# Second mixer's pairs: outputs summed with channels in partitions, and the small inverse as a product of crossed powers

## The chip, the cores and the metric

One core of one Trainium2 chip. The metric is the device time of one execution of the whole program, in microseconds (us). Between kernels the medians of repeated executions are compared.

## The reference, cut to what matters

The program is two blocks. The change lies in the second block's first mixer, a recurrence over 512 tokens in 16 heads of 64 channels, with one 64x64 state for each head:

```python
def rwkv7_time_mix(xn, mu, w_in, w0, w1, w2, a0, a1, a2, k_k, k_a, r_k, lnx_g, lnx_b, w_out):
    ...
    def step(state, inp):
        r_t, w_t, k_t, v_t, kk_t, a_t = inp
        s_kk = jnp.einsum('bhij,bhj->bhi', state, kk_t)
        state = (state * w_t[:, :, None, :]
                 - s_kk[..., None] * (kk_t * a_t)[:, :, None, :]
                 + v_t[..., None] * k_t[:, :, None, :])
        return state, jnp.einsum('bhij,bhj->bhi', state, r_t)
    ...
    mean = jnp.mean(y, axis=-1, keepdims=True)
    var = jnp.mean(jnp.square(y - mean), axis=-1, keepdims=True)
    y = ((y - mean) * lax.rsqrt(var + GN_EPS) * lnx_g.astype(f32).reshape(H, N)
         + lnx_b.astype(f32).reshape(H, N))
    y = y + jnp.sum(r * k * r_k.astype(f32), axis=-1, keepdims=True) * v
    y = y.reshape(B, S, D).astype(xn.dtype) * jax.nn.silu(g)
    return y @ w_out
```

## The kernel before, in words

The kernel takes the heads two at a time: eight **pairs** `p` of 128 channels. Within a pair the tokens are cut into eight **chunks** of 64. Inside a chunk the recurrence is turned into matrix products, which needs the inverse of a 64x64 triangular matrix for each chunk and head, 16 to a pair. The state passes from chunk to chunk.

A tile of 16 such 64x64 matrices has 128 partitions and eight blocks of 64 columns. The upper and the lower 64 partitions are the even and the odd chunk of two, and a block is one head of such a two. All products of such tiles are float32, 64 rows deep and 64 columns wide, so that one takes a quarter of the array of TensorE. There are two kinds:

- `blocks_pe` (line 2758): 16 products, each from upper half to upper half or from lower to lower. They land in one PSUM bank. Only two of the four quarters of the array are used.
- the crossed kinds, `to_heads_pe` (2776), `from_heads_pe` (2788), `TaT_pe` (2999) and `channels_pe` (2800): 16 products that go from chunk halves to head halves or back, by turns in all four quarters. They land in two banks.

For each pair the steps are, by their names in the code:

1. `C1`, `C2`, `MT` (line 2800) and VectorE's masks (`mask_dve`, 3478) that take them to `M`, `qb`, `qk`, `ak`, `MT`, `O16` and `O32`.
2. The inverse of the 16x16 diagonal blocks by squaring: `N` and `NT` (second powers), `MT2` and `M2` (fourth), `NT3` (eighth), each a `blocks_pe` that ScalarE copies to SBUF (3166). Each power is multiplied onto the running `X` by `X0`, `X1`, `X2`, also `blocks_pe`, and added to `X` by VectorE (`add_X_dve`, 3562). Then `T16`, `G16`, `A16` and `T32`, `G32`, `A32` widen the inverse to 32 and to 64.
3. `WX`, `Wv`, `TaT`: what the state is multiplied with.
4. The recurrence, for each chunk `c`: `from_state_pe` (3015, 3017) reads the state `St`; VectorE makes `nU` (3584) and copies the part of the output that comes from the state into `yt` (3595); `to_state_pe` (3032, 3034) makes the update; VectorE scales the old state (`SP`, 3605) and forms the new one (`S`, 3615).
5. `inside_pe` (3050, 3053): the rest of the output of all eight chunks, 32 small products in a row into bank 7, with tokens in partitions. `inside_dve` (3754) adds it to `yt`, `turn_y_pe` transposes the sum (4 transposes, 288), and `yf_act` (3398) copies it.
6. `mean` (3072), `dv` (3764), `y2` (3406), `var` (3080), then `sd`, `normed` (3773), `gain` (3432), `add_bonus` (3782), `out` (3791).

The order of the work is written out by hand, one list for each engine: `pair_pe`, `pair_act` and `pair_dve`, called for `s` from 0 to 10. They interleave the pairs. Between `TaT` of one pair and `TaT` of the next, TensorE carries the eight chunks of pair `s - 1`, and between its two halves of every chunk one step of item 1 or 2 for pair `s`; then it goes on to `inside`, `T16`, and so on. A **from `TaT` to `TaT`** stretch is called an interval here; there are seven. Before the first one only pair 0's matrices are made. After the last one `EarlyOut` fills the gaps of pair 7's chunks with matmuls of the output projection (3921), and what is left of them follows.

Each engine runs its list in order. A wait (`wait_ge`) holds all that stands behind it on that engine. `K.bank(b, ...)` lets TensorE wait until the last reader of a PSUM bank is done. For instance `N` waits for `O32`, the last reader of `MT` in banks 0 and 1, and `tal` and `tka` wait for whoever reads their bank before.

Of the kernel before, what the change touches and what calls it, by code (L numbers as in the profile page):

```python
# [2685 lines left out]
class Pairs:  # L2686
    def __init__(self, K):
        blocks = lambda: K.carve(8, HEAD)
        two = lambda: [blocks() for _ in range(2)]
        self.nU, self.yt = two(), two()  # L2690
# [179 lines left out]
def NT_pe(K, X, q, p):  # L2870
# [4 lines left out]
    blocks_pe(K, q, p, "NT", X.M, X.MT, q.act)  # L2875


def X0_pe(K, X, q, p):
    if outside(p):
        return  # L2880
    K.nc.tensor.wait_ge(*q.act.at("NT read", p))
    K.nc.tensor.wait_ge(*q.dve.at("X start", p))
    blocks_pe(K, q, p, "X0", X.NT, X.X, q.dve)


def M2_pe(K, X, q, p):
# [4 lines left out]
    blocks_pe(K, q, p, "M2", X.NT, X.N, q.act)  # L2891


def MT2_pe(K, X, q, p):
# [4 lines left out]
    blocks_pe(K, q, p, "MT2", X.N, X.NT, q.act)  # L2899


def X1_pe(K, X, q, p):
    if outside(p):
        return
    K.nc.tensor.wait_ge(*q.act.at("MT2 read", p))
    K.nc.tensor.wait_ge(*q.dve.at("X0 read", p))
    blocks_pe(K, q, p, "X1", X.MT, X.X, q.dve)
# [1922 lines left out]
```

## Time and profile before

| | us |
|---|---|
| median of 3 executions | 2651.22 (2648.41 to 2654.54) |
| profiled execution, its own time | 2643.84 |
| its span | 2642.2 |
| TensorE (PE) busy in the span | 2504.9 (95%) |
| first `C2` of pair 0 to `TaT` of pair 0 | 1832.30 to 1855.02 |
| the seven intervals | 1855.02 to 2081.45 |
| from there to the end of the early output matmuls | 2081.45 to 2126.5 |

The stretch that the change touches is thus some 295 us of 2642. In the rows PE is TensorE's matmuls, DVE is VectorE, ACT is ScalarE. A float32 matmul is recorded as two, so that a product of 16 shows as x32.

### The profile page before, as it was taken

How to read it: one execution, taken by the hardware profiler on the slowest of the kernel's cores; microseconds unless marked ns; L12 is line 12 of the kernel's file. 1: busy time of each engine (PE TensorE's matmuls, PEld its weight loads, DVE VectorE, ACT ScalarE, POOL GpSimd, SP SyncE). 2: the span in 40 equal slices, each digit the busy share in tenths (PEclk: the TensorE clock that was granted, in tenths of full speed). 3: DMA queues.
4: the chain of work that ended last, by engine and by line, in shares of the span. 5: the costliest groups of instructions: out<-in, count | busy, mean ns of one | idle time of the engine just before them, and what ended most of it. 6: DMA issues, size and time to landing. Idle time of an engine off the chain costs nothing. (4 is left out here: it accounts for less than half of the span.)

```text
span 2642.2 us, 43397 instructions
## 1 busy us (share of the span) xinstructions
PE 2504.9 (95%) x17508; PEld 1694.5 (64%) x17508; DVE 1295.2 (49%) x2714; ACT 678.5 (26%) x1184; POOL 166.2 (6%) x128
## 2 busy tenths in 40 slices
PE   8999999999999899899998989999999899999997
PEld 3666676488874667666665644865777645677644
DVE  4656656567653222122121127622787535666625
ACT  2333233101112111111111111023455323333422
POOL 0000000000000012222222210000000000000000
PEclk9999999999999899999999999999999999999999
DMA  6222112244342598999999882342111142111120
GB/s 276 113 80 96 64 48 76 92 167 182 121 158 80 233 370 320 387 335 395 381 347 394 311 326 98 100 183 97 34 62 34 54 171 74 64 57 57 64 76 32
DMA packets 83733, 436.54 MB, mean 165 GB/s; under 512 B 16432, under 2 KB 16944, under 8 KB 39888
## 3 DMA queue, kind: packets, MB, share of 16 engines
q1 hardware_dynamic: 54592, 372.92, 35.8%
q0 software_dynamic: 18096, 37.80, 5.6%
q10 hardware_dynamic: 10848, 23.04, 2.4%
q8 instruction: 141, 2.31, 0.4%
q14 instruction: 56, 0.46, 0.0%
HBM read 400.59 MB, written 61.41 MB: 175 GB/s over the span
## 5 line engine op out<-in xcount | busy, mean ns | idle before, releaser
L278 PE MATMUL psum_all<-u,weights 128*128 128x512 f32 x704 | 306.9, 593 | 0.0
L278 PEld LDWEIGHTS psum_all<-u,weights 128*128 128x128 f32 x704 | 132.4, 190 | 157.7 <-issue 157.3
L958 PE MATMUL psum_all<-big,weights 128*128 128x256 f32 x928 | 214.7, 381 | 2.1 <-ACT sq L1015 1.3
L1892 PE MATMUL psum_all<-big 128*32 128x256 f32 (+2 forms) x1648 | 195.1, 382 | 6.0 <-DMA big<-t_experts 4.5
L958 PEld LDWEIGHTS psum_all<-big,weights 128*128 128x128 f32 x928 | 174.5, 190 | 34.2 <-issue 5.1
L1892 PE MATMUL psum_all<-weights,big 128*64 128x256 f32 (+2 forms) x1296 | 187.9, 388 | 8.4 <-DMA weights<-t_experts 8.4
L958 PE MATMUL psum_all<-big 128*128 128x256 f32 x784 | 179.0, 379 | 0.0
L1892 PEld LDWEIGHTS psum_all<-big 128*32 128x32 f32 (+2 forms) x1648 | 138.1, 132 | 39.0 <-issue 8.8
L958 PEld LDWEIGHTS psum_all<-big 128*128 128x128 f32 x784 | 148.7, 190 | 22.4 <-DVE big L946 0.8
L1892 PEld LDWEIGHTS psum_all<-weights,big 128*64 128x64 f32 (+2 forms) x1296 | 131.2, 145 | 48.8 <-issue 15.4
L1927 DVE COPY big<-psum_all 128x256 f32<-128x256 f32 x46 | 19.5, 424 | 279.1 <-PE psum_all L288 279.1
L278 PE MATMUL psum_all<-weights,u 128*128 128x256 f32 x640 | 139.6, 379 | 0.0
L278 PEld LDWEIGHTS psum_all<-weights,u 128*128 128x128 f32 x640 | 121.5, 190 | 19.9 <-issue 3.8
L1902 ACT ACTIVATE big<-psum_all 128x256 f32<-128x256 f32 x46 | 17.7, 385 | 442.2 <-PE psum_all L1892 421.1
L1939 PE MATMUL psum_all<-weights,big 128*32 128x512 f32 (+2 forms) x440 | 110.3, 633 | 12.7 <-DMA weights<-t_experts 7.5
L288 PE MATMUL psum_all<-const_cols,big 128*128 128x128 f32 (+2 forms) x748 | 108.2, 278 | 11.5 <-DMA big<-u_rows,rows 5.7
L278 PEld LDWEIGHTS psum_all<-big 128*128 128x128 f32 x568 | 78.8, 198 | 61.1 <-issue 50.3
L288 PEld LDWEIGHTS psum_all<-const_cols,big 128*128 128x128 f32 (+2 forms) x748 | 84.1, 141 | 46.4 <-issue 21.7
L278 PE MATMUL psum_all<-big 128*128 128x3 f32 (+4 forms) x568 | 92.0, 289 | 12.7 <-issue 5.6
L1939 PE MATMUL psum_all<-big 128*64 128x512 f32 (+2 forms) x296 | 95.8, 627 | 8.2 <-DMA big<-t_experts 6.8
L1961 DVE COPY big<-psum_all 128x512 f32<-128x512 f32 x35 | 24.2, 691 | 150.7 <-PE psum_all L1939 120.7
L2457 PE MATMUL psum_all<-big,weights 128*128 128x512 f32 x192 | 83.0, 592 | 3.6 <-DVE big L2611 3.6
(475 smaller groups left out, 4013.7 us busy)
## 6 DMA issues: line engine op xcount, KB each, us to landing
big<-t_experts SPq DMA_DIRECT2D x96, 1024.0 KB
weights<-t_experts SPq DMA_DIRECT2D x96, 1024.0 KB
weights<-t_ada SPq DMA_DIRECT2D x24, 1024.0 KB, 7.0
weights<-t_rkvg SPq DMA_DIRECT2D x16, 1024.0 KB, 8.6
rwkv_inputs<-big ACTq DMA_DIRECT2D x48, 256.0 KB, 2.3
big<-rwkv_inputs SPq DMA_DIRECT2D x8, 1280.0 KB, 6.8
weights<-t_x SPq DMA_DIRECT2D x8, 1024.0 KB, 4.9
weights<-t_BC SPq DMA_DIRECT2D x8, 1024.0 KB, 4.9
```

What stands on the lines that cost most here:

```text
L278: last = pe.matmul(out, lhsT, rhs, start=n == 0, stop=n == len(terms) - 1)
L288: last = K.nc.tensor.transpose(out, a, K.c("ident")[0:a.shape[0], 0:a.shape[0]])
L958: ins = pe.matmul(out, w[:, k, :], x[:, k, :], start=first and k == 0, stop=k == n - 1, skip_group_check=not first)
L1892: ins = pe.matmul(K.psum[rows, bank, n * F_E:(n + 1) * F_E], xT[:, k, rows], X.part(r, n, KD, F_E)[:, k, :], start=k == 0, stop=k == KD - 1)
L1902: act.activation(X.act[b % 2], K.psum[:, b % 2, 0:F_E], ACT.Silu).then_inc(*q.act.tick("gate", b))
L1927: dve.tensor_copy(X.hidT[b % 2].rearrange("p a b -> p (a b)"), K.psum[:, 4, 0:F_E]).then_inc(*q.dve.tick("hidT", b))
L1939: ins = pe.matmul(K.psum[rows, 2 + half, :], X.hidT[b % 2][:, j, rows], X.part(r, 2, 2, D)[:, j, half * 512:half * 512 + 512], start=j == ...
L1961: dve.tensor_copy(X.y[e % len(X.y)][:, 512:1024], K.psum[:, 3, :]).then_inc(*q.dve.tick("y", e))
L2457: ins = pe.matmul(K.psum[:, j % 4, :], K.W.tile(w, KD, 256)[:, k, j % 2 * P:(j % 2 + 1) * P], X.mix[c][:, k, :], start=k == 0, stop=k == K ...
```

## The change

Three things are changed.

**Outputs.** `yt`, its eight copies, `inside_dve` and `turn_y` go. `from_state_pe` makes the output's part with the operands swapped, so that channels are in partitions, straight into bank 6 (`Y_BANK`), and leaves the sum open. `inside_pe` now runs for each chunk, behind `to_state`, and adds its four products to it. Chunk 7's stands at the head of the next step. The update of the state moves from bank 6 to a part of bank 4. `from_state_pe` has two signals in place of one ("from S" after the first two products, "y from S" after the other two), and TensorE now also waits for two signals of its own: "y" of the chunk before and "y from S".

**Inverse.** In place of three additions of `power * X` it is a product: `P = (1 + M4)(1 + M)`, `Q = (1 + N) P`, `X = (1 + M8) Q`, where `A2`, `A4` and `A8` are the powers with the unit matrix added by VectorE. `N`, `NT`, `MT2`, `M2`, `NT3`, `P` and `X` are of the crossed kind, `Q` is `blocks_pe`.

**Order.** `WX` moves from chunk 2 to chunk 4, and its read behind `N`'s; `qb` moves behind `MT` on VectorE; on ScalarE `yf` and `gain` now stand behind `X`'s read and ahead of `T16`'s.

```diff
@@ class Pairs
-        self.nU, self.yt = two(), two()
+        self.nU = two()
@@
-        self.alt, self.Wv, self.WX = blocks(), blocks(), blocks()
+        self.alt, self.Wv, self.WX, self.A2, self.A4 = (blocks() for _ in range(5))
@@
-               "C2": 0, "C1": 2, "MT": 0, "WX": 2, "NT": 3, "N": 0, "X0": 1, "MT2": 2, "M2": 3,
-               "X1": 0, "NT3": 1, "tal": 2, "tka": 3, "X2": 0}
+               "C2": 0, "C1": 2, "MT": 0, "NT": 2, "N": 0, "WX": 2, "MT2": 0, "M2": 2,
+               "P": 0, "NT3": 2, "tal": 1, "Q": 0, "tka": 1, "X": 2}
@@ N_pe, NT_pe; M2_pe and MT2_pe likewise with from_heads_pe
-    blocks_pe(K, q, p, "N", X.MT, X.M, q.act)
+    to_heads_pe(K, q, p, "N", X.MT, X.M, q.act)
@@
+def P_pe(K, X, q, p):
...
+    for name in ("X start", "A4"):
+        K.nc.tensor.wait_ge(*q.dve.at(name, p))
+    to_heads_pe(K, q, p, "P", X.A4, X.X, q.act)
+def Q_pe(K, X, q, p):
...
+    K.nc.tensor.wait_ge(*q.act.at("P read", p))
+    K.nc.tensor.wait_ge(*q.dve.at("A2", p))
+    blocks_pe(K, q, p, "Q", X.A2, X.N, q.act)
+def X_pe(K, X, q, p):
...
+    K.nc.tensor.wait_ge(*q.act.at("Q read", p))
+    K.nc.tensor.wait_ge(*q.dve.at("NT3 read", p))
+    from_heads_pe(K, q, p, "X", X.M, X.NT, q.act)
@@ from_state_pe
+        K.bank(Y_BANK, q.act, "yf", p)
...
-        pe.matmul(K.psum[rows, 4 + h, 0:HEAD], chunk(X.TaT, c)[half(h), :], X.St[half(h), :], start=True, stop=True)
+        ins = pe.matmul(K.psum[rows, 4 + h, 0:HEAD], chunk(X.TaT, c)[half(h), :], X.St[half(h), :], start=True, stop=True)
+    ins.then_inc(*q.pe.tick("from S", p, c))
+    if c > 0:
+        pe.wait_ge(*q.pe.at("y", p, c - 1))
     for h in range(2):
-        ins = pe.matmul(K.psum[rows, 4 + h, HEAD:P], al_rh(X, p, c)[half(h), 1, :], X.St[half(h), :], start=True, stop=True)
-    ins.then_inc(*q.pe.tick("from S", p, c))
+        ins = pe.matmul(chunk(K.psum[half(h), Y_BANK, :], c), X.St[half(h), :], al_rh(X, p, c)[half(h), 1, :], start=True, stop=False)
+    ins.then_inc(*q.pe.tick("y from S", p, c))
@@
-def inside_pe(K, X, q, p):
+def inside_pe(K, X, q, p, c):
...
+    pe.wait_ge(*q.dve.at("nU", p, c))
+    pe.wait_ge(*q.pe.at("y from S", p, c))
+    for h in range(2):
+        pe.matmul(chunk(K.psum[half(h), Y_BANK, :], c), X.nU[n][rows, 2 * t + h, :], X.qb[n][rows, 2 * t + h, :],
+                  start=False, stop=False)
+    for h in range(2):
+        ins = pe.matmul(chunk(K.psum[half(h), Y_BANK, :], c), X.vt[n][rows, 2 * t + h, :], X.qk[n][rows, 2 * t + h, :],
+                        start=False, stop=True)
+    ins.then_inc(*q.pe.tick("y", p, c))
-def turn_y_pe(K, X, q, p):
...
@@ VectorE: A2_dve; A4_dve alike from X.MT; yt_dve and inside_dve are removed
+    dve.wait_ge(*q.act.at("NT read", p))
...
+    dve.tensor_tensor(X.A2, X.NT, K.c("eye64").unsqueeze(1).to_broadcast([P, 8, HEAD]), ALU.add).then_inc(*q.dve.tick("A2", p))
+def A8_dve(K, X, q, p):
...
+    dve.wait_ge(*q.pe.at("NT3", p))
+    dve.tensor_tensor(heads_first(X.M), crossed(K, "NT3"), K.c("eye64").unsqueeze(1).unsqueeze(1).to_broadcast([P, 2, NT, HEAD]),
+                      ALU.add).then_inc(*q.dve.tick("NT3 read", p))
@@ pair_act
-    NT3_act(K, X, q, s - 1)
-    expn_act(K, X, q, s)
+    P_act(K, X, q, s - 1)
     rate_act(K, X, q, s)
     tal_act(K, X, q, s - 1)
+    Q_act(K, X, q, s - 1)
+    expn_act(K, X, q, s)
+    tka_act(K, X, q, s - 1)
+    X_act(K, X, q, s - 1)
+    yf_act(K, X, q, s - 2)
     gain_act(K, X, q, s - 3)
-    tka_act(K, X, q, s - 1)
+    T16_act(K, X, q, s - 1)
+    G16_act(K, X, q, s - 1)
     expp_act(K, X, q, s)
-    T16_act(K, X, q, s - 1)
-    yf_act(K, X, q, s - 2)
-    G16_act(K, X, q, s - 1)
     y2_act(K, X, q, s - 2)
@@ pair_dve, the middle
-    add_X_dve(K, X, q, s - 1, "X0")
+    A2_dve(K, X, q, s - 1)
     S_dve(K, X, q, s - 2, 5)
-    scan_dve(K, X, q, s)
+    A4_dve(K, X, q, s - 1)
     nU_dve(K, X, q, s - 2, 5)
     SP_dve(K, X, q, s - 2, 5)
...
+    scan_dve(K, X, q, s)
+    S_dve(K, X, q, s - 2, 6)
+    SP_dve(K, X, q, s - 2, 6)
+    A8_dve(K, X, q, s - 1)
     ends_dve(K, X, q, s - 1)
```

The order on TensorE at chunks 6 and 7. Before (2758 is `NT3`, 3015 and 3017 `from_state`, 288 `tal` and `tka`, 3032 and 3034 `to_state`, 2758 again `X2`, and 3050 and 3053 the first of the eight like pairs of rows of `inside`):

```order
L2758 MATMUL psum_all<-weights 64x64 x16
L3015 MATMUL psum_all<-big 64x64 x2
L3017 MATMUL psum_all<-big 64x64 x2
L288 MATMUL psum_all<-const_cols,big 128x128 x4
L3032 MATMUL psum_all<-big 64x64 x2
L3034 MATMUL psum_all<-big 64x64 x2
L288 MATMUL psum_all<-const_cols,big 128x128 x4
L3015 MATMUL psum_all<-big 64x64 x2
L3017 MATMUL psum_all<-big 64x64 x2
L2758 MATMUL psum_all<-weights 64x64 x16
L3050 MATMUL psum_all<-big,weights 64x64 x2
L3053 MATMUL psum_all<-big,weights 64x64 x2
```

The same place after the change, from `tal` on (3019 and 3024 are `from_state`, 3039 and 3041 `to_state`, 3057 and 3060 `inside`, 288 `tal` and `tka`, 2758 `Q`, 2788 `X`):

```order
L288 MATMUL psum_all<-const_cols,big 128x128 x4
L3039 MATMUL psum_all<-big 64x64 x2
L3041 MATMUL psum_all<-big 64x64 x2
L3057 MATMUL psum_all<-weights,big 64x64 x2
L3060 MATMUL psum_all<-weights,big 64x64 x2
L2758 MATMUL psum_all<-weights,big 64x64 x16
L3019 MATMUL psum_all<-big 64x64 x2
L3024 MATMUL psum_all<-big 64x64 x2
L288 MATMUL psum_all<-const_cols,big 128x128 x4
L2788 MATMUL psum_all<-weights 64x64 x16
L3057 MATMUL psum_all<-weights,big 64x64 x2
L3060 MATMUL psum_all<-weights,big 64x64 x2
```

The last step of the small inverse is now a crossed product, and one chunk's `inside` stands in front of `T16` where all eight stood.

ScalarE at the same place, before (3166: read of `tal`; 3432 `gain`; 3166 read of `tka`; 3350 `expp`; 3166 read of `T16`; 3398 `yf`; 3173 read of `G16`; 3406 `y2`):

```order
L3166 ACTIVATE big<-psum_all 128x512
L3432 ACTIVATE big<-big,vector_cols 128x512
L3166 ACTIVATE big<-psum_all 128x512
L3350 ACTIVATE big<-big 128x512
L3166 ACTIVATE weights<-psum_all 128x512
L3398 ACTIVATE big<-psum_all 128x512
L3173 ACTIVATE weights<-psum_all 128x2x4x64
L3406 ACTIVATE big<-big 128x512
```

and after (reads of `tal` and `Q`, 3378 `expn`, reads of `tka` and `X`, 3415 `yf`, 3449 `gain`, reads of `T16` and `G16`, 3367 `expp`, 3423 `y2`):

```order
L3170 ACTIVATE big<-psum_all 128x512
L3170 ACTIVATE weights<-psum_all 128x512
L3378 ACTIVATE big<-big 128x512
L3170 ACTIVATE big<-psum_all 128x512
L3177 ACTIVATE weights<-psum_all 128x2x4x64
L3415 ACTIVATE big<-psum_all 128x512
L3449 ACTIVATE big<-big,vector_cols 128x512
L3170 ACTIVATE weights<-psum_all 128x512
L3177 ACTIVATE weights<-psum_all 128x2x4x64
L3367 ACTIVATE big<-big 128x512
L3423 ACTIVATE big<-big 128x512
```

`gain` moved from ahead of `tka`'s read to behind `X`'s read and `yf`, and three reads (`Q`, `tka`, `X`) with `expn` between stand ahead of it.

## Rows read from the trace of the kernel before

**Rows 1.** The page's first line.

```profile
span 2642.2 us, 43397 instructions
```

**Rows 2.** Busy time by stretch: four of the seven intervals; after the comma PE, PEld, DVE, ACT.

```profile
1855.02:1886.83 31.81, 29.60 (x796) 24.26 (x797) 24.25 (x59) 15.79 (x28) 0.00 (x0) 1.00 0.13 45
...
1918.98:1950.88 31.90, 29.78 (x797) 24.48 (x797) 26.23 (x62) 17.12 (x30) 0.00 (x0) 1.00 0.16 53
1950.88:1984.00 33.12, 29.91 (x796) 24.45 (x797) 26.46 (x62) 17.11 (x30) 0.00 (x0) 1.00 0.15 51
...
2049.27:2081.45 32.18, 28.39 (x790) 23.81 (x791) 22.58 (x56) 12.81 (x22) 0.00 (x0) 1.00 0.20 72
```

**Rows 3.** Timeline of TensorE, third interval: start, us, line, shapes, idle before.

```profile
1918.98 0.69 PE L2999 MATMUL psum_all<-weights,big 64*64 64x64 f32 x32 [0.32 <-ACT big L3388]
1919.47 1.13 PE L2758 MATMUL psum_all<-big,weights 64*64 64x64 f32 x32
1920.44 0.33 PE L3015 MATMUL psum_all<-big 64*64 64x64 f32 x4
...
1922.67 0.33 PE L3032 MATMUL psum_all<-big 64*64 64x64 f32 x4 [0.64 <-DVE big L3595]
...
1922.99 1.10 PE L2800 MATMUL psum_all<-big 64*64 64x128 f32 x32
1924.05 0.33 PE L3015 MATMUL psum_all<-big 64*64 64x64 f32 x4
...
1924.29 0.69 PE L2800 MATMUL psum_all<-big 64*64 64x64 f32 x32
1925.30 0.33 PE L3032 MATMUL psum_all<-big 64*64 64x64 f32 x4 [0.31 <-DVE big L3584]
...
1941.26 0.66 PE L288 MATMUL psum_all<-const_cols,weights 128*128 128x128 f32 x4
1942.20 0.63 PE L288 MATMUL psum_all<-const_cols,big 128*128 128x128 f32 x4 [0.28 <-DVE big L3754]
1942.76 0.69 PE L2776 MATMUL psum_all<-weights 64*64 64x64 f32 x32
...
1946.15 1.13 PE L3080 MATMUL psum_all<-big,const_cols 128*128 128x512 f32 x2 [0.38 <-ACT big L3406]
```

**Rows 4.** Groups of instructions by line and form, the pairs' stretch.

```profile
L3166 ACT ACTIVATE weights<-psum_all 128x512 f32<-128x512 f32 x56 | 33.5, 598 | 40.1 <-PE psum_all L2758 26.8 <-PE psum_all L3017 6.8 <-PE psum_all L288 6.2
...
L3595 DVE COPY big<-psum_all 64x128 f32<-64x128 f32 x64 | 18.1, 282 | 0.5
...
L3630 DVE TENSOR_TENSOR_SCAN big<-big 128x512 f32<-128x512 f32 x7 | 8.5, 1214 | 0.0
```

**Rows 5.** Timeline of ScalarE and of VectorE, third interval, the output's tail.

```profile
1939.84 0.82 ACT L3432 ACTIVATE big<-big,vector_cols 128x512 f32<-128x512 f32 x1 [0.99 <-DVE big L3773]
...
1941.97 0.68 DVE L3782 TENSOR_TENSOR big<-big 128x512 f32<-128x512 f32 x1
1942.76 0.69 DVE L3791 TENSOR_TENSOR u<-big 128x512 f32<-128x512 f32 x1
1943.37 0.69 DVE L3657 TENSOR_TENSOR big<-big 128x512 f32<-128x512 f32 x1
1944.75 0.69 DVE L3764 SCALAR_TENSOR_TENSOR big<-psum_all,big 128x512 f32<-128x512 f32 x1 [0.69 <-PE psum_all L3072]
```

**Rows 6.** Timeline of TensorE, the first pair before any recurrence.

```profile
1847.42 0.63 PE L288 MATMUL psum_all<-const_cols,weights 128*128 128x128 f32 x4 [0.88 <-DVE weights L3562]
```

**Rows 7.** Timeline of TensorE, pair 7's last chunk and what follows.

```profile
2099.40 0.33 PE L3015 MATMUL psum_all<-big 64*64 64x64 f32 x4
...
2100.48 0.33 PE L3050 MATMUL psum_all<-big,weights 64*64 64x64 f32 x4 [0.63 <-DVE big L3595]
...
2102.49 1.12 PE L3921 MATMUL psum_all<-u,weights 128*128 128x512 f32 x2
...
2108.35 18.19 PE L3921 MATMUL psum_all<-u,weights 128*128 128x512 f32 x42
```

More of the change, by code:

```diff
@@ L2874, in NT_pe @@
         K.nc.tensor.wait_ge(*q.dve.at(name, p))
[L2875 to L2883, printed above, removed]
+    to_heads_pe(K, q, p, "NT", X.M, X.MT, q.act)
 def M2_pe(K, X, q, p):
@@ L2898, in MT2_pe @@
         K.nc.tensor.wait_ge(*q.act.at(name, p))
[L2899 to L2907, printed above, removed]
+    from_heads_pe(K, q, p, "MT2", X.N, X.NT, q.act)
 def NT3_pe(K, X, q, p):
@@ L2935, in G16_pe @@
         return
-    for name in ("O16", "X2 read"):
-        K.nc.tensor.wait_ge(*q.dve.at(name, p))
-    to_heads_pe(K, q, p, "G16", X.O16, X.X)
+    K.nc.tensor.wait_ge(*q.dve.at("O16", p))
+    K.nc.tensor.wait_ge(*q.act.at("X read", p))
+    to_heads_pe(K, q, p, "G16", X.O16, X.X, q.act)
 def A16_pe(K, X, q, p):
@@ L3058, in turn_y_pe @@
-def turn_y_pe(K, X, q, p):
-    if outside(p):
-        return
-    K.nc.tensor.wait_ge(*q.dve.at("y", p))
-    K.bank(7, q.act, "yf", p)
-    transposes(K, [(tile(K.psum[:, 7, :], t), X.yt[p % 2].rearrange("p b n -> p (b n)")[:, t * P:(t + 1) * P]) for t in range(NT)]) \
-        .then_inc(*q.pe.tick("turn y", p))
+    pe, n, rows, t = K.nc.tensor, p % 2, half(c % 2), c // 2
+    if c == 0:
+        pe.wait_ge(*q.act.at("tv read", p))
+        for name in ("qb", "qk"):
+            pe.wait_ge(*q.dve.at(name, p))
@@ L3123, in pair_pe @@
     to_state_pe(K, X, q, s - 1, 0)
+    inside_pe(K, X, q, s - 1, 0)
     early.pe(s == KD, 1)
@@ L3238, in MT2_act, with P_act, Q_act, X_act @@
         K.nc.scalar.wait_ge(*q.pe.at(name, p))
-    take_act(K, q, p, "MT2", X.MT)
-def NT3_act(K, X, q, p):
+    take_crossed_act(K, q, p, "MT2", X.MT)
+def P_act(K, X, q, p):
     if outside(p):
         return
-    for name in ("X0", "MT2", "M2"):
+    for name in ("M2", "MT2"):
         K.nc.scalar.wait_ge(*q.pe.at(name, p))
-    take_act(K, q, p, "NT3", X.NT)
+    take_crossed_act(K, q, p, "P", X.N)
+def Q_act(K, X, q, p):
+    if outside(p):
+        return
+    K.nc.scalar.wait_ge(*q.dve.at("A2", p))
+    take_act(K, q, p, "Q", X.NT)
+def X_act(K, X, q, p):
+    if outside(p):
+        return
+    K.nc.scalar.wait_ge(*q.pe.at("P", p))
+    take_crossed_act(K, q, p, "X", X.X)
 def T16_act(K, X, q, p):
@@ L3252, in T16_act @@
         return
-    for name in ("X1", "NT3"):
-        K.nc.scalar.wait_ge(*q.pe.at(name, p))
+    K.nc.scalar.wait_ge(*q.pe.at("NT3", p))
+    K.nc.scalar.wait_ge(*q.dve.at("A4", p))
     take_act(K, q, p, "T16", X.MT)
@@ L3585, in nU_dve @@
                              X.Wv[rows, 2 * t:2 * t + 2, :], ALU.mult, ALU.subtract).then_inc(*q.dve.tick("nU", p, c))
-def yt_dve(K, X, q, p, c):
-    if outside(p):
-        return
-    dve, rows, t = K.nc.vector, half(c % 2), c // 2
-    if c == 0 and p >= 2:
-        dve.wait_ge(*q.pe.at("turn y", p - 2))
-    dve.wait_ge(*q.pe.at("from S", p, c))
-    dve.tensor_copy(X.yt[p % 2][rows, 2 * t:2 * t + 2, :], K.psum[rows, 4:6, HEAD:P]).then_inc(*q.dve.tick("from S read", p, c))
 def SP_dve(K, X, q, p, c):
@@ L3711, in rh_dve @@
     if p >= 2:
-        for key in (("C1", p - 2), ("C2", p - 2), ("from S", p - 2, 7)):
+        for key in (("C1", p - 2), ("C2", p - 2), ("y from S", p - 2, 7)):
             dve.wait_ge(*q.pe.at(*key))
```

150 lines of the change are left out of this document (68 added, 82 removed).

## The prediction

> **What bounds the kernel now.** I read the page first for the span [rows 1], then the busy time by stretch [rows 2], then the timelines of the three engines over one clean interval [rows 3, 5], and the groups of instructions [rows 4] for what one costs. The change touches only the pairs, so the question is what sets the length of an interval. In the third one, 31.90 us long, TensorE is busy 29.78, VectorE 26.23 and ScalarE 17.12 [rows 2]. The clock is granted in full (1.00). TensorE's idle time is a handful of short waits: 0.64 and 0.31 for VectorE in chunks 0 and 1, 0.28 for `inside_dve`, 0.38 for `y2`, 0.32 ahead of `TaT` [rows 3]. So TensorE's list is the bound, with VectorE 3.5 us behind it. The fourth interval is 1.2 us longer with the same busy time [rows 2]: gaps in issuing that wait for no engine. I leave those as they are. The profiled execution took 2643.84 us against a median of 2651.22; I work out a difference and take it off the median.
>
> **TensorE's sum.** Starts give the price of a product. `TaT`, crossed, lets the next start after 1919.47 - 1918.98 = 0.49; `Wv`, of the blocks kind, after 1920.44 - 1919.47 = 0.97 [rows 3]. Both hold the same 16 products. In an interval:
> - `X0`, `X1`, `X2` go: 3 x 0.97 = 2.91.
> - `N`, `NT`, `MT2`, `M2`, `NT3` become crossed: 5 x 0.48 = 2.40.
> - `P`, `X` (0.49 each) and `Q` (0.97) come: 1.95.
> - `turn_y` goes: 1942.76 - 1942.20 = 0.56 [rows 3].
> - `inside` took 2102.49 - 2100.48 = 2.01 in one run [rows 7]. As eight pieces, each costs what four small products cost in front of a like-shaped one, 1924.29 - 1924.05 = 0.24 [rows 3], so 1.9 to 2.1: nothing either way.
>
> Together -3.9 us. VectorE loses three additions, `inside_dve` and eight copies of 0.28 [rows 4], which stand 0.2 apart, and gains `A2`, `A4`, `A8`: about -2.3. ScalarE loses one read and gains three of 0.60 [rows 4], +1.2. If busy time decided, an interval would fall to 28 us.
>
> **Why it will not.** A crossed product takes 0.49, its read 0.60 on ScalarE [rows 3, 4]; until now a product of 0.97 covered it. The chain now also runs through more hands: `MT2` read, `A4`, `P`, its read, `Q`, its read, `X`, its read, `T16`. I walked the new lists through the third interval with the rows' durations: 0.61 from the start of one 512-wide VectorE operation to that of the next, 0.79 where it needs the result of the one before [rows 5], 0.5 between ScalarE's reads, and about 0.05 from an end to the start that waits. Times from `TaT`:
> - `to_state` 0 stays at 3.69; VectorE's list ahead of it is unchanged [rows 3].
> - `inside` 0 pushes `C1` from 4.01 to 4.21. `M` and `nU` 1 follow `C1`, so `to_state` 1 goes from 6.32 [rows 3] to 6.50: the first waits are not shortened.
> - `to_state` 2 at 8.95 waits for `nU`, behind `MT`'s and `qb`'s masks; `WX` no longer covers it.
> - `N` must wait for `O32` to leave banks 0 and 1: 10.40. `to_state` 4 comes at 13.1.
> - `P` waits for `A4`, behind `WX`'s, `kk2`'s and `MT2`'s reads on ScalarE: 15.1, after some 0.7 idle.
> - The scan (1.21 [rows 4]) and `A8` now stand ahead of `nU` 6: `to_state` 6 at 18.1.
> - `Q` 18.6, `from_state` 7 at 19.5, `tka` 19.8, `X` 20.45 (it waits for `Q`'s read). `X`'s read is behind `expn` and `tka`'s read: 21.3 to 21.9. `T16` starts at 21.95, before at 1941.26 - 1918.98 = 22.28.
>
> So of 3.9 us some 0.3 arrive at `T16`. Then the output's tail decides. After `X`'s read ScalarE does `yf` (0.5) and `gain` (0.82 [rows 5]), to 23.15. `add_bonus`, `out`, `k2`, `dv` follow on VectorE, whose starts lie 0.79, 0.61 and 0.61 apart [rows 5] (before, `dv` had to wait for `mean`; here `mean` is done first): `dv` ends at 25.9, `y2` at 26.55, and `var` starts at 26.62. Before, it started at 1946.15 - 1918.98 = 27.17 [rows 3]. From `var` to the next `TaT` the lists are as they were: 4.73, TensorE's own work. New interval: 31.35, **-0.55**.
>
> The other pieces. The first interval has no `gain`, `add_bonus` and `out`, so `dv` follows `mean` at once: -1.35. The last has no `k2`, and `gain` weighs as before: -1.15. Pair 0 before its `TaT` has no state work to cover anything, and is a chain of reads: by the same walk `T16` starts at 1847.9 instead of 1847.42 [rows 6], +0.5. At the end, pair 7's chunks grow by 0.1 each (`inside` stands on the way, `nU` may start 0.12 earlier), +0.7, and behind them 2.01 of `inside` become 0.3, `turn_y` goes, and the wait for `yt`'s copy shortens: the last run of output matmuls starts 1.65 earlier than 2108.35 [rows 7], and they are TensorE's own time.
>
> Sum: +0.5 - 1.35 - 5 x 0.55 - 1.15 - 1.65 = -6.4. From 2651.22: **2644.8 us**. Per interval the unknown is large beside its value: one operation more or less in the chain is 0.6. Ends: all of TensorE's 3.9 arrives, or `T16` comes 0.6 later and nothing does.
>
> A rule that speaks against the change: the Trainium skill, "TensorEngine Tiling (Array Packing)", section "PSUM Bottleneck", says that splitting the array speeds up TensorE but not the emptying of PSUM, which may then become the limit. By that rule the 3.9 us are not to be had, and the walk agrees; without it the intervals alone would give -27.
>
> **Rivals.**
> 1. *TensorE stays the bound.* The reads fit behind `inside`'s pieces after all. For it: VectorE has 2.3 us less to do, ScalarE is half idle [rows 2]. Against: the chain above, and that each engine takes its list in order. 7 x -3.9, and -1.65 at the end: about -29, 2622. Something halfway, -1.5 in each, gives 2638. Together 0.13.
> 2. *No change to measure.* The chain to `T16` is one operation (0.6) longer than I walk it, say because `A4` or `A8` slips behind the scan's turn. Then the intervals give nothing and only the ends help: -2 to -3, 2649. Chance 0.25.
> 3. *Slower: TensorE waits for itself.* Before, it never waited for its own signals here. Now each chunk has two, "y" of the chunk before and "y from S". The trace shows no such wait; a lower bound is nothing, since one product lies between the signal and the wait in nearly all cases; an upper one is what the last of a run of small products takes from its start to its end, 0.22 (the 0.69 of a set against its 0.49 spacing [rows 3]), and the signal's way of 0.05. 15 waits x 0.27 = 4 us in each pair, +26 in all with the gain taken off: 2677. At a third of it, 2655.5. It turns the sign from 0.05 us in a wait on (6.4 over 8 pairs and 15 waits). Chance 0.13, since the products that stand between last longer than 0.27.
> 4. *The crossed order does not run in four quarters for these tiles.* Then 7 products cost 0.48 more each and all waits behind them too; TensorE's sum is -0.6 and the sign turns. Against: `N` uses the very loop of `G16`. Chance 0.02.
>
> The Trainium skill, "TensorE: Matmul & The Clock Gate", section "The cost: per-tile semaphore tail", has increments serialize, some 26 ns for each. The change adds 14 signals to a pair. By that page alone this would be an estimate of +3 us in all and bring the sum to -3.4; the trace has no pair of places that differ in their signals alone, so the sum leaves it out. It would add to rival 3.
>
> **The numbers.** About 0.2% (5.3 us) is what a measurement of this kernel can tell from no change. My forecast is 2644.8 with a chance of 0.47, spread over -3 to -11: its middle is just beyond the bound, so some 0.41 of it and all of rival 1 are faster (0.54). The other 0.06, rival 2 and a quarter of rival 3 are within it (0.34), the rest of rival 3 and rival 4 slower (0.12). The range goes from halfway to rival 1's milder case and beyond to rival 3 at a third and the medians' own spread: 2631 to 2656.
>
> **What would show it.** Right: the intervals with about 31.3 us and TensorE busy some 26 in them; waits of TensorE for ScalarE's reads ahead of `P` and `T16`, for VectorE ahead of `N`; `dv` started by VectorE's own list and not by `mean`; `var` the only late step after it. `turn_y` gone and the run after `var` earlier by 1 to 2. Wrong in favour: intervals under 30. Wrong against: idle time of TensorE at lines 3024 and 3057 with no other engine named, or `inside`'s pieces over 0.3 each.

## The result: slower, 1.0067 times the kernel before, and the profile after

Measured together, 11 executions of each: **2673.59 us** (median, 2659.59 to 2679.14) against 2652.0 before. The ratio is 1.0067, 95% interval 1.0045 to 1.0089: slower by 0.45 to 0.9%. The forecast was 2644.8, the range ended at 2656, and slower had a chance of 0.12. Both kernels' executions fall into a faster and a slower group, of the changed kernel five from 2659.6 to 2664.4 (mean clock 0.981 to 0.983) and six from 2673.6 to 2679.1 (0.975 to 0.978), of the kernel before eight from 2644.1 to 2654.5 and three from 2659.7 to 2666.3. Like against like the change costs 13.2 and 15.6 us (by the medians); the rest of the 21.6 us between the kernels' medians comes of more executions with the lower mean clock. The profiled one took 2678.32, so its rows show that lower clock too, while the profile before is of an execution of 2643.84; the difference of the two spans, 34.8 us, is larger than that of the medians.

The page's first line, answering to [rows 1]:

```profile
span 2677.0 us, 43365 instructions
```

Busy time by stretch after, columns as in [rows 2]: five of the seven intervals, and two stretches behind the last `TaT`.

```profile
1858.82:1896.40 37.58, 29.07 (x792) 23.42 (x793) 21.95 (x50) 16.88 (x30) 0.00 (x0) 0.91 0.11 38
1896.40:1931.21 34.81, 28.34 (x792) 22.65 (x793) 23.71 (x53) 17.66 (x32) 0.00 (x0) 0.95 0.14 48
1931.21:1965.08 33.87, 27.05 (x793) 21.54 (x793) 23.89 (x53) 17.88 (x32) 0.00 (x0) 1.00 0.15 50
1965.08:1997.87 32.79, 26.93 (x792) 21.21 (x793) 23.86 (x53) 17.65 (x32) 0.00 (x0) 1.00 0.15 52
2065.81:2099.44 33.63, 25.54 (x786) 20.59 (x787) 20.24 (x47) 13.68 (x24) 0.00 (x0) 1.00 0.17 61
2099.44:2120.00 20.56, 17.66 (x190) 10.31 (x192) 3.54 (x14) 1.71 (x3) 0.00 (x0) 0.60 0.17 72
2120.00:2130.00 10.00, 9.46 (x61) 4.58 (x58) 1.89 (x7) 0.00 (x0) 0.00 (x0) 0.50 0.01 2
```

TensorE's work did fall: 27.05 busy in the third interval where there were 29.78 [rows 2]. The interval still grew, from 31.90 to 33.87. Where it went, stretch by stretch (own sums of the timeline's idle times; "gaps" are those that end with `issue`, so that no engine and no transfer is named):

| stretch | before | after | difference |
|---|---|---|---|
| first `C2` to `TaT` of pair 0 | 22.72 | 23.58 | +0.86 |
| the seven intervals | 226.43 | 240.62 | +14.2 |
| of this, gaps | 2.8 | 17.1 | +14.3 |
| last `TaT` to the end of the early output matmuls | 45.0 | 58.5 | +13.5 |

The rest of the 34.8 us between the spans lies outside the stretch the change touches: pair 0's `C2` began 2.9 later, and what follows the early output matmuls took 3.3 longer.

That the gaps alone come to just the whole loss of the intervals is in part chance. Less its gaps, each of the last five intervals is as long as before or shorter (by 0.5 on average), and the first two, in which the clock fell, are 1.5 and 0.8 longer; together 223.56 against 223.67.

The timeline of TensorE after, third interval (columns as in [rows 3]; 3039 is now `to_state`, 3019 `from_state`, 2776 and 2788 the crossed kinds). The rows are picked, and what stands between them is left out:

```profile
1931.21 0.69 PE L2999 MATMUL psum_all<-weights,big 64*64 64x64 f32 x32 [0.32 <-ACT big L3405]
1934.90 0.33 PE L3039 MATMUL psum_all<-big 64*64 64x64 f32 x4 [0.64 <-DVE big L3628]
1937.88 0.33 PE L3039 MATMUL psum_all<-big 64*64 64x64 f32 x4 [0.61 <-DVE big L3628]
1940.36 0.33 PE L3039 MATMUL psum_all<-big 64*64 64x64 f32 x4 [0.36 <-DVE big L3628]
1942.15 0.69 PE L2776 MATMUL psum_all<-weights 64*64 64x64 f32 x32 [0.30 <-DVE big L3628]
1945.10 0.27 PE L3019 MATMUL psum_all<-big 64*64 64x64 f32 x2 [0.86 <-issue]
1947.59 0.68 PE L2776 MATMUL psum_all<-weights,big 64*64 64x64 f32 x28 [0.25 <-DVE big L3585]
1949.37 0.33 PE L2776 MATMUL psum_all<-weights,big 64*64 64x64 f32 x4 [1.10 <-issue]
1955.65 0.65 PE L288 MATMUL psum_all<-const_cols,weights 128*128 128x128 f32 x4 [0.57 <-ACT weights L3177]
1960.35 1.13 PE L3078 MATMUL psum_all<-big,const_cols 128*128 128x512 f32 x2 [1.30 <-ACT big L3423]
```

Two rows are new in this interval: 0.86 and 1.10 us in which nothing is waited for. The second cuts a product in two, after 28 of its 32 records, where no wait stands. Such rows lie about 123 recorded matmuls apart, or a multiple of that (some records are missing from a trace). They are in every interval after, two or three in each; before, only three of the seven had any, the longest this one:

```profile
2006.65 0.27 PE L3053 MATMUL psum_all<-big,weights 64*64 64x64 f32 x2 [0.74 <-issue]
```

The trace also has the times of every transfer. A packet of 16 KB on the instruction queue lands 1.3 to 1.6 us ahead of the end of each of these gaps: of all 17 after, up to the one in the tail (for 1945.10 it landed at 1943.74, for 1949.37 at 1947.98), and of all six before. So in both kernels TensorE starts again when a block of instructions has come.

What one operation takes did not change (598 ns for a read of ScalarE's before [rows 4]):

```profile
L3177 ACT ACTIVATE weights<-psum_all 128x512 f32<-128x512 f32 x57 | 34.1, 599 | 70.6 <-PE psum_all L2776 49.0 <-PE psum_all L3019 14.6 <-PE psum_all L2788 5.6
```

The output's tail in that interval, ScalarE and VectorE, answering to [rows 5] (3449 `gain`, 3807 `add_bonus`, 3816 `out`, 3691 `k2`, 3789 `dv`, 3423 `y2`):

```profile
1955.96 0.83 ACT L3449 ACTIVATE big<-big,vector_cols 128x512 f32<-128x512 f32 x1
...
1956.82 0.69 DVE L3807 TENSOR_TENSOR big<-big 128x512 f32<-128x512 f32 x1 [2.22 <-ACT big L3449]
1957.62 0.69 DVE L3816 TENSOR_TENSOR u<-big 128x512 f32<-128x512 f32 x1
1958.23 0.69 DVE L3691 TENSOR_TENSOR big<-big 128x512 f32<-128x512 f32 x1
1958.94 0.69 DVE L3789 SCALAR_TENSOR_TENSOR big<-psum_all,big 128x512 f32<-128x512 f32 x1
...
1959.67 0.63 ACT L3423 ACTIVATE big<-big 128x512 f32<-128x512 f32 x1 [1.39 <-DVE big L3789]
```

TensorE's timeline at the worst gap, in the first interval, and then busy time by stretch around it (last three columns: granted clock, DMA share, GB/s):

```profile
1879.25 0.70 PE L2776 MATMUL psum_all<-weights,big 64*64 64x64 f32 x15 [3.37 <-issue]
```

```profile
1873.00:1878.00 5.00, 2.17 (x102) 1.97 (x95) 3.52 (x8) 2.79 (x5) 0.00 (x0) 1.00 0.61 243
1878.00:1883.00 5.00, 3.75 (x77) 3.30 (x78) 1.50 (x5) 1.30 (x2) 0.00 (x0) 0.51 0.01 3
```

The gap of 3.37 begins at 1875.88, in the 1.28 MB load of the next pair's inputs, which the first row below shows for 1872 to 1877, without a packet of instructions beside it. The next such packet came at 1877.02 (second row, 1876.9 to 1878.1), when the load was over:

```profile
q1 hardware_dynamic: 141, 1.31, 71.5%
...
q8 instruction: 1, 0.02, 4.9%
```

From 1878 to 1883 the mean granted clock is 0.51; the lower of its two levels is 1.2 GHz, 0.50. The tail's timeline has two idle times close together:

```profile
2102.32 0.33 PE L3039 MATMUL psum_all<-big 64*64 64x64 f32 x4 [0.97 <-ACT big L3441]
2103.60 0.37 PE L3057 MATMUL psum_all<-weights,big 64*64 64x64 f32 x3 [0.83 <-issue]
2104.22 2.07 PE L3937 MATMUL psum_all<-u,weights 128*128 128x512 f32 x2
```

An idle time of 0.97 and one of 0.83, beside the loads for the output matmuls; then a mean clock of 0.60 up to 2120, of 0.50 up to 2130, and one 512-wide matmul takes 2.07 instead of 1.12 [rows 7]. Before, the clock was 1.00 there.

### The profile page after: what moved, and what is told of

Same layout as the page of the kernel before. It is cut to its first block, busy times and chain, and to the rows that moved or that the text cites. A ratio compares the mean times of both kernels' runs of the same rounds, so it can differ in the third digit from the quotient of the medians.

```text
span 2677.0 us, 43365 instructions
## 1 busy us (share of the span) xinstructions
PE 2504.4 (94%) x17476; PEld 1681.6 (63%) x17476; DVE 1275.7 (48%) x2642; ACT 684.7 (26%) x1200; POOL 166.1 (6%) x128
## 4 chain that ended last, share of the span: by engine, by line
PE 78%; DMA 10%; DVE 6%; issue 3%; ACT 2%; SPq 0%; POOL 0%; ACTq 0%; DVEq 0%; POOLq 0%
PE psum_all L278 24%; PE psum_all L958 17%; PE psum_all L1892 8%; DMA big<-t_experts 4%; PE psum_all L1939 4%; PE psum_all L2457 3%; PE psum_all L288 3%; PE psum_all L4202 2%; PE psum_all L1421 2%; PE psum_all L3937 2%; DMA total_rows<-big,rows 1%; DMA weights<-t_experts 1%; DMA weights<-t_ada 1%; PE psum_all L3995 1%; PE psum_all L717 1%
## 5 line engine op out<-in xcount | busy, mean ns | idle before, releaser
L288 PE MATMUL psum_all<-const_cols,big 128*128 128x128 f32 (+2 forms) x716 | 104.3, 280 | 10.5 <-DMA big<-u_rows,rows 6.5
```

Source lines behind the costliest of these rows:

```text
L288: last = K.nc.tensor.transpose(out, a, K.c("ident")[0:a.shape[0], 0:a.shape[0]])
```

## The experiments

Two theories at the start. **A**: instructions reach TensorE at a limited rate; the crossed products consume them twice as fast as before and run the store dry. **B**: TensorE waits for its own signals (rival 3), and the trace names nobody for it. Ratios are to the kernel before, run together with each set: its medians were 2649.73 beside experiments 1, 2, 3 and 5, 2651.07 beside 4, 6, 7 and 8, and 2652.63 beside 9 to 11.

**1. Forty products in a row, nothing to wait for.**

```diff
+    for _ in range(20): 16 crossed products, operands A2 and A4
+    for _ in range(20): 16 products of the blocks kind
```

> The changed kernel, with 20 crossed sets of 16 products and then 20 sets of the blocks kind put in one row behind X of pair 0, in free banks, waiting for nothing; the outputs are not touched. Theory A (the supply of instructions): the changed kernel's gaps at which TensorE waits for no engine (17 us over seven intervals, 2.8 before) are TensorE out of instructions: crossed products are used up faster than they come. Then the crossed row has gaps every 128 recorded matmuls and takes clearly over its own 20 x 0.48 = 9.6 us, some 15 to 21, while the blocks row (20 x 0.95 = 19.0) has hardly any. Theory B (the gaps come from the waits for TensorE's own signals in each chunk): no wait stands in the rows, so no gap: 9.6 and 19.0 us.

Measured: 2707.4 us. TensorE's timeline of the row (3108 crossed, 3113 blocks):

```profile
1849.73 2.09 PE L3108 MATMUL psum_all<-big 64*64 64x64 f32 x127 [0.66 <-issue]
1853.44 2.09 PE L3108 MATMUL psum_all<-big 64*64 64x64 f32 x128 [1.63 <-issue]
1856.91 2.09 PE L3108 MATMUL psum_all<-big 64*64 64x64 f32 x128 [1.38 <-issue]
1860.93 2.09 PE L3108 MATMUL psum_all<-big 64*64 64x64 f32 x128 [1.93 <-issue]
1864.68 2.09 PE L3108 MATMUL psum_all<-big 64*64 64x64 f32 x128 [1.65 <-issue]
...
1868.70 19.18 PE L3113 MATMUL psum_all<-big 64*64 64x64 f32 x640
```

And the transfers of that stretch, 1850 to 1870:

```profile
q8 instruction: 5, 0.08, 1.5%
```

128 records are 256 instructions, as each has its load of weights. TensorE runs them in 2.09 us and then has none. A group begins 3.71, 3.47, 4.02, 3.75 and 4.02 us behind the one before it, 3.79 on average, so that the 20 crossed sets took 19.0 us and not 9.6. In this stretch the instruction queue moves five packets of 16 KB and no other queue anything. So with all else quiet TensorE gets 256 instructions in 3.79 us, 14.8 ns for each. By the transfers' own times each of these packets starts 1.0 to 1.7 us behind the start of the group before, takes about 1 us, and the next group starts 1.4 to 1.6 us behind its landing: the limit here is how long it takes to get a block, not what the queues can move (the packets take 1.5% of the DMA engines' time). The blocks kind takes 0.97 for 64 instructions [rows 3], 15.2 ns, and its 640 records ran in 19.18 us without a gap: it just keeps below the supply. The crossed kind takes 0.49, 7.7 ns. Theory A is shown as to the gaps; there are no signals in the row, which B needs.

**2 and 3. Each half of the change alone.**

```diff
 outputs alone: yt, inside_dve and turn_y go, inside_pe per chunk; the inverse and all orders as before
 inverse alone: P, Q, X in place of three additions, seven crossed products, order of WX; outputs as before
```

> The new outputs alone, the small inverse as before. Theory A: TensorE's pace stays as it was (blocks products), so gaps stay near before's 0 to 1.2 us an interval; per interval the sum saves turn_y and a wait, the chunks are 0.25 longer: intervals 31.5 to 32.5, whole program within 5 us of before. Theory B (own signals): gaps of 2 us an interval as in the changed kernel, and 10 to 20 us slower than before. Theory C (the clock): pair 7's chunks are alike in this kernel and in the changed one, so where their lower granted clock comes from the chunks' own waits it is here too, +12 us; where it needs a gap in instructions at the start of them, it is not.

Measured: 2650.57 against 2649.73, ratio 1.0011 (0.9995 to 1.0027), no change. In the tail the clock stayed at 1.00, so the chunks' own waits (0.97 ahead of the first `to_state` here too) do not bring it down by themselves, against theory C's first half.

> The crossed inverse alone, the outputs as before (yt, inside in one run, turn_y); gain and yf stand on ScalarE where before has them. Theory A: gaps of 1.5 to 3 us an interval as in the changed kernel; intervals 32 to 34; whole program 5 to 15 us slower than before. Theory B: hardly any gap, intervals of 31 or less, faster than before by 5 to 10.

Measured: 2677.78, ratio 1.011 (1.0095 to 1.0126), 28 us slower where 5 to 15 were expected, with intervals of 34.6 to 38.1 where 32 to 34 were. The loss is the inverse's, but only part of it is the supply's: the seven intervals took 254.2, 27.7 more than before, and their gaps 10.5, 7.7 more. The second has no gap at all, a clock of 1.00, less TensorE work than before, and is still 2.4 longer. Its busy time, and the longest wait in it, which is that of `X` for `Q`'s read:

```profile
1898.92:1933.51 34.59, 28.12 (x796) 21.89 (x797) 25.77 (x62) 18.08 (x32) 0.00 (x0) 1.00 0.15 49
...
1921.41 0.69 PE L2788 MATMUL psum_all<-weights 64*64 64x64 f32 x32 [2.06 <-ACT weights L3166]
```

`gain` stands ahead of `Q`'s read here, as in experiment 8, which has the same wait. So with the old orders the product form loses by waits; the whole change, with `gain` moved, loses less.

The outputs alone gained nothing in the intervals (227.4 against 226.43; gaps 2.4) and 1.1 in the tail. They have all 15 waits for TensorE's own signals in each pair; no idle time in the intervals is put down to them, the gaps did not grow, and the interval of the ratio ends 7 us above no change: rival 3's price of 26 is refuted. A cost of a few hundredths of a us in each wait, and the 3 us that the prediction gave as an estimate for 14 more signals in a pair, cannot be told from nothing. What the outputs freed on TensorE turned into two waits:

```profile
1913.43 0.63 PE L288 MATMUL psum_all<-const_cols,weights 128*128 128x128 f32 x4 [0.72 <-DVE weights L3566]
...
1915.37 1.13 PE L3070 MATMUL psum_all<-big,const_cols 128*128 128x512 f32 x2 [0.69 <-ACT big L3402]
```

`T16` waits 0.72 for `X2`'s addition, which `inside` used to cover, and `mean` waits 0.69 for `yf`, which ScalarE does behind `T16`'s read.

**4. The changed kernel with the seven crossed products made blocks again.**

```diff
-    to_heads_pe(K, q, p, "N", X.MT, X.M, q.act)
+    blocks_pe(K, q, p, "N", X.MT, X.M, q.act)
...
```

> The changed kernel with N, NT, MT2, M2, NT3, P and X of the blocks kind again (two quarters of the array), reads and the unit matrix's addition to match; order and outputs as changed. TensorE's own sum is 7 x 0.47 = 3.3 us an interval longer. Theory A (supply): gaps fall from 2 us an interval to under 0.7, so that an interval grows by less than 1.5 or not at all, and the clock stays up; whole program 2650 to 2665, no slower than the changed kernel. Theory B (waits, not supply): gaps stay and intervals grow by some 3 us: 2685.

Measured: 2667.29 (2662.15 to 2676.93), ratio 1.0052 (1.0034 to 1.0071). Gaps fell from 17.1 to 5.3 us, and the tail's clock was 1.00. The ratio cannot be told from that of the changed kernel (1.0045 to 1.0089), and half of the gaps that are left, 2.73 us, is one in the first interval, where the clock is 0.95. A gap-free interval:

```profile
1932.75:1965.92 33.17, 28.89 (x792) 23.77 (x793) 23.97 (x53) 17.88 (x32) 0.00 (x0) 1.00 0.15 51
```

It is 1.3 longer than one with the old inverse (31.85, below at experiments 9 to 11). The two kernels differ in the form of the inverse and in the orders. So the product form with its orders costs 1.3 in each interval when it isn't crossed; that this is because its products are links of the chain up to `T16`, where the additions were VectorE's beside it, is my reading: TensorE's waits for ScalarE are 2.14 in this interval and 1.39 in the other. Crossing them takes the third interval without its gaps to 33.87 - 1.96 = 31.91, and brings gaps of 1.75 to 4.28 in each. The two nearly cancel. So taking away nearly all gaps this way did not win the time back: without crossing, the product form is slower than before as well, and no run here has crossed products without gaps.

**5 and 6. The inputs of pairs 2 to 7 loaded as a sliver, twice.** The kernel leaves out most of what these pairs load, and its result is not the program's.

```diff
+            if p < 2: sp.dma_start(X.ins[p % 2], scratch[p, :, 0:5, :])
+            else:     sp.dma_start(X.ins[p % 2][:, 0:1, 0:HEAD], scratch[p, :, 0:1, 0:HEAD])
```

> The changed kernel with the pairs' inputs loaded in full for pairs 0 and 1 only; from pair 2 on a load brings 64 columns of one input (the rest of the computation of the mixer thus works on old values). Theory A with the loads as its aggravation: the first interval's gap of 3.37 us, which fell together with a load of 1.25 MB, goes (interval 1 at 34 or less instead of 37.6), the gaps of about 1 us elsewhere stay where no load was beside them. If all gaps are from loads, intervals fall to 31.5. If loads have nothing to do with it, interval 1 keeps a gap of over 2 us.

> The kernel of e4 once more, one look at its clock and its first interval: the gap of instructions in the first interval stays under 2.5 us where the changed kernel had 4.3, and interval 1 is near 33.4.

Measured: 2673.47, ratio 1.0096 (1.0078 to 1.0115), and 2671.23 the second time. The first interval fell from 37.58 to 33.35, its gaps from 4.28 to 2.27 and its clock rose from 0.91 to 1.00 (second: 33.08, gaps 2.01). The load had made the gap longer. The other intervals had gaps of 1.5, 2.24, 0.46, 1.9, 2.7 and 2.59, only the fourth clearly less than with the loads (1.75): the load is not what makes them. The seven intervals took 234.2 instead of 240.6. In the tail idle times of 0.97 and 0.60 stood 0.4 us apart, the clock was low again (mean 0.73 from the last `TaT` to the end of the early output matmuls), and the tail took 56.9. The median of its four executions, 2673.47, is that of the changed kernel, as all four had a low mean clock (0.973 to 0.978).

**7. The loads for the output matmuls sent before pair 7's inputs**, so in the sixth interval and not behind the last `TaT`.

```diff
     for p in range(KD + 1):
+        if p == KD - 1:
+            early_loads()
```

> The changed kernel, with the three 1 MB loads of the output projection's weights issued on SyncE's queue ahead of pair 7's inputs instead of behind all pairs' loads, so that they are done before TaT of pair 7; nothing else. Theory D (the low clock of pair 7's chunks is set off by TensorE running dry there: 0.97 us for ScalarE and a gap of 0.83 us in its instructions beside these loads): no gap of 0.8 us at chunk 0, the clock stays at 1.00 in the tail, and all executions lie near 2660 instead of near 2660 or near 2677. Theory E (the chunks of pair 7 as such are too thin for the full clock, whatever the gap): both groups of times stay.

Measured: 2666.31 (2659.74 to 2683.54), ratio 1.0048 (1.0026 to 1.007). No gap in the tail, its clock 1.00, its length 44.4 instead of 58.5. So theory D holds for the tail, but not for the executions: eight ended below 2669 and four above 2672. The profiled one, of 2672.80, had the gap elsewhere. Its timeline and its busy time in the sixth interval:

```profile
2043.88 0.47 PE L2800 MATMUL psum_all<-big 64*64 64x64 f32 x4 [2.52 <-issue]
```

```profile
2035.31:2073.96 38.65, 31.72 (x793) 25.56 (x793) 23.88 (x53) 17.68 (x32) 0.00 (x0) 0.82 0.20 77
```

The gap grew where the loads went, to 2.52 (the longest there was 1.28), and the interval's clock is 0.82. What the tail gave, this took back in part.

**8. `gain` back behind `tal`'s read, where it stood before.**

```diff
     tal_act(K, X, q, s - 1)
+    gain_act(K, X, q, s - 3)
     Q_act(K, X, q, s - 1)
```

> The changed kernel with gain put back on ScalarE behind tal's read, ahead of Q's, where before has it; nothing else. Theory G (the chain gain, add_bonus, out, k2, dv, y2 sets var): TensorE's wait of 1.30 us ahead of var falls to 0.4, intervals 2 to 6 are 0.7 to 0.9 shorter, whole program about 4 us faster than the changed kernel. If instruction supply alone sets the interval, the time shows up in a gap elsewhere, and the intervals stay.

Measured: 2680.96, ratio 1.0099 (1.0068 to 1.013). The wait ahead of `var` fell to 0.38, as theory G has it, but the time is a miss: no gain, and intervals of 250.7 in all where the changed kernel had 240.6. TensorE's timeline, then ScalarE's, in the third interval:

```profile
1960.68 0.70 PE L2788 MATMUL psum_all<-weights 64*64 64x64 f32 x32 [1.75 <-ACT weights L3170]
```

```profile
1959.33 0.81 ACT L3449 ACTIVATE big<-big,vector_cols 128x512 f32<-128x512 f32 x1 [2.49 <-DVE big L3798]
1960.05 0.57 ACT L3170 ACTIVATE weights<-psum_all 128x512 f32<-128x512 f32 x1
```

`gain` waits 2.49 for `normed`, and `Q`'s read stands behind it on the same engine, so `X` waits 1.75. The order of the change was right here: in the product form `Q`'s read on ScalarE is on the chain.

**9 to 11. Outputs alone, and what they freed collected.** Three steps, each with the ones before it:

```diff
 9: ScalarE
-    expp_act, T16_act, yf_act, G16_act
+    yf_act, T16_act, G16_act, expp_act
 10: TensorE
-    tka_pe ahead of from_state_pe of chunk 7
+    tka_pe between inside_pe of chunk 7 and T16_pe
 11: VectorE
-    M_dve, nU_dve of chunk 1
+    nU_dve of chunk 1, M_dve
```

> The outputs alone, and on ScalarE `yf` stands ahead of T16's read and `expp` behind G16's. In the run with the outputs alone, `mean` waited 0.69 us for `yf`, and T16 0.72 for VectorE's last addition. Theory A (what the outputs saved was handed to ScalarE's order): `mean` starts 0.85 earlier, `dv`, `y2` and `var` 1.0 earlier, a clean interval falls from 32.0 to about 31.0, the whole by some 6 us to 2644. Theory B (ScalarE's order is neutral, the next thing in the chain is VectorE's `k2`, or the masks): interval within 0.3 of 32.0, 2650.

> As the run before, and `tka` moves on TensorE from ahead of chunk 7 to behind its `inside`, so that it covers the wait of T16 for the last addition (0.72). Theory A: T16 starts some 0.6 earlier, but `yf` is held by ScalarE's own list (`gain`, `tka` read), so `mean` gains only 0.15 more: interval 30.9, whole 2643. Theory B: `tka`'s read now holds `gain` and `yf` up, and the move gives it back: no better than the run before.

> As the run before, and VectorE's `nU` of chunk 1 stands ahead of the mask `M`. The wait of `to_state` 1 is 0.61 in every interval, after `M`. Theory A: `to_state` 1 comes 0.4 earlier and all behind it: -0.4 in each of seven intervals, -2.8 us on the run before. Theory B: `MT`'s product and its mask come later by what `nU` takes (0.3), `nU` 2 and 3 stand behind them, and the wait appears one or two chunks later: within 1 us of the run before.

| | us | ratio, 95% interval |
|---|---|---|
| 9 | 2646.45 | 0.9971 (0.995 to 0.9991) |
| 10 | 2644.47 | 0.9964 (0.9947 to 0.998) |
| 11 | 2642.37 | 0.996 (0.9941 to 0.998) |

Busy time in a gap-free interval (the fifth) of the outputs alone, of experiment 9 and of experiment 11, in this order:

```profile
1988.88:2020.73 31.85, 28.50 (x792) 23.64 (x793) 23.96 (x53) 16.78 (x30) 0.00 (x0) 1.00 0.15 53
```

```profile
1987.71:2019.18 31.47, 28.65 (x793) 23.75 (x793) 23.98 (x53) 16.89 (x30) 0.00 (x0) 1.00 0.16 53
```

```profile
1983.54:2014.14 30.60, 28.80 (x792) 23.93 (x793) 23.80 (x53) 16.90 (x30) 0.00 (x0) 1.00 0.17 56
```

In 9 the wait of `mean` is gone (0.69), but the interval gave 0.38 and not 1.0: in the chunks, one product of the blocks kind stretched from 1.03 to 1.42, with no wait named. In 11 both waits and that of `to_state` 1 are gone (its timeline of TensorE, `to_state` 1, `T16` and `mean`):

```profile
1989.40 0.33 PE L3039 MATMUL psum_all<-big 64*64 64x64 f32 x4
...
2005.66 0.63 PE L288 MATMUL psum_all<-const_cols,weights 128*128 128x128 f32 x4
...
2006.85 1.12 PE L3070 MATMUL psum_all<-big,const_cols 128*128 128x512 f32 x2
```

The waits that VectorE ends fell from 1.97 to 0.84 in an interval. By the 95% intervals neither 10 nor 11 is told apart from 9; against the kernel before, each is faster, and 11 by 0.2 to 0.6%. It beats both kernels. Its seven intervals took 219.7, those of the outputs alone 227.4.

## Why the prediction was wrong, point by point

- **The step that failed** is in the first part: "gaps in issuing that wait for no engine. I leave those as they are." They were the trace's sign that the supply of instructions is nearly used up: each of the six ended 1.35 to 1.50 us behind the landing of a block of instructions. A row that I quoted holds the rest: 0.97 us for 64 instructions of the blocks kind, 0.49 for the crossed kind. I priced a crossed product at 0.49 wherever it stands. It has this price only until the 256 instructions at hand are used up. The gaps went from 2.8 to 17.1 us, +14.3, against an interval gain of 5.25 that was forecast. That without them the sign would have been the forecast one is a subtraction, and not a run.
- **The clock**, which I took as 1.00, is the second. It fell in interval 1 (0.91), in the gap of 3.37; in interval 2 (0.95), behind idle times of 0.54 and 1.17, 0.3 us apart; and in the tail. The length of an idle time does not decide it alone: gaps of 1.28 and 1.25 in intervals 6 and 7 left it at 1.00. In the tail of the profiled execution this and the 0.83 gap come to +13.5, where I had -1.65. Without the fall (experiment 7) the tail took 44.4 against 45.0: -0.6.
- TensorE's sum held in its sign: -3.9 was forecast (some 26 busy), 29.78 - 27.05 = 2.7 less is busy.
- **The walk.** `to_state` 0 came at 3.69 (3.69 forecast), 1 at 6.67 (6.50), 2 at 9.15 (8.95), `N` at 10.94 (10.40), `T16` at 24.44 (21.95), of which 1.96 are the two gaps. From `T16` to `var` it was 4.70 (4.67), from there to `TaT` 4.73 (4.73), with `y2` behind `gain`, `add_bonus`, `out`, `k2`, `dv`, as walked. What is left of the error is 0.5, all of it there by `N`, whose wait ends by the trace behind `nU` of chunk 3 and not behind `O32`. Without its gaps the third interval thus gained nothing (31.91 against 31.90). Less their gaps, intervals 3 to 6 are 0.39 shorter on average, where I had -0.55, and the seventh 0.88, where I had -1.15; the first, forecast at -1.35, is 1.5 longer. The walk's mechanism was right for the last five, its gain somewhat too large, under gaps of some 2 us in each. (A gap can cover a wait, so the remainder is a lower bound of what an interval without gaps would take.)
- Pair 0 ahead of its `TaT`: +0.86, forecast +0.5. Its `T16` stood 15.12 behind `C2` before [rows 6] and now 15.95, by the row below; the wait for `X`'s read ahead of it is 0.80.

```profile
1851.19 0.66 PE L288 MATMUL psum_all<-const_cols,weights 128*128 128x128 f32 x4 [0.80 <-ACT weights L3177]
```

- **The page I weighed**, the Trainium skill, "TensorEngine Tiling (Array Packing)", section "PSUM Bottleneck", says that the emptying of PSUM may become the limit when the array is split. The trace agrees as far as this: the chain through the reads held back most of what TensorE saved (`T16` waited 0.57 for `X`'s read), and experiments 3 and 8 show it with waits of 2.06 and 1.75 for `Q`'s. But the split products met another limit too, the supply of instructions, and its 14.3 us are what the forecast lacked.
- **Rival 1** (TensorE stays the bound): no. **Rival 2**: its condition, `T16` 0.6 later than walked, nearly held in the third interval (0.5 without the gaps), but the whole was not "no change". **Rival 3** had the sign and nearly the size (2677) with the wrong mechanism: idle times stand at 3024 and 3057 among others, but at places without signals too, and the outputs alone carry all the signals at no cost that shows. That its 2677 is near 2673.59 is luck. I gave the right sign 0.12, and no case for the right cause. **Rival 4**: no, the crossed products run in 0.49.
- Left open: why the clock fell in some executions and not in others. The kernel before does it as well: 7 of its 23 executions beside experiment 7 and 8 of 28 beside 9 to 11 had a mean clock of 0.974 to 0.979 and took 2659.8 to 2668.2, the others 0.981 to 0.985 and at most 2655.3. Nor does the pair of idle times settle it: 0.97 and 0.60 in the tail of experiment 5 went with a low clock, 0.97 and 0.63 in that of experiment 10, 2.9 us of work and one short wait apart, with 1.00. No profile of a changed kernel's execution with the higher mean clock was taken, so the tail's +13.5 stands for the others alone. Nor was the changed kernel tried with its inputs loaded in smaller pieces, or the small inverse with only some of its products crossed.

## What to carry to other kernels

Before you make small matmuls faster, divide the new time by the number of instructions and hold it against the rate at which the trace shows them arriving: here 256 in 3.79 us, so float32 products of 64x64 in two quarters were already at the limit, and a row of such in four quarters stood idle after every 256 instructions, four sets of 16. An idle time that waits for nothing can be a resource near its end: look at what else arrived just before it ended, and do not carry it over as a constant. And when a change frees an engine without moving the time, look at which wait took its place: the new outputs alone changed nothing (2650.57), and with four operations of ScalarE in another order they took 2646.45, whose interval lies below no change.

## What the runs showed of the hardware

- Instructions came to TensorE in blocks of 256, one 16 KB packet each, at 14.8 ns for an instruction with all other queues quiet (experiment 1), and TensorE started again 1.3 to 1.6 us behind a packet's landing. Beside a load (243 GB/s in those 5 us) one packet came only when the load was over, and TensorE stood idle 3.37 us; with the load gone the interval's gaps were 2.27 in place of 4.28.
- With an idle time of 3.37 us the granted clock went from 1.00 to its lower level (0.51 over 5 us), though the engine had work from then on, and behind idle times of 0.97 and 0.83 close together it was low over most of the 30 us from the last `TaT` (0.60, then 0.50). Single gaps of 1.25 and 1.28 left it at 1.00.
